# A straight-line schedule for a diffusion block: two heads projected inside the first stage, heads two deep, Fourier products between halves of the output projection

## What is computed

```python
sh1, sc1, gt1, sh2, sc2, gt2 = modulation(c, w_ada[l], b_ada[l])
csh1, csc1, ...              = modulation(c_ctx[None], w_ada[l], b_ada[l])
hc = modulate(rms_norm(ctx, g_mix_pre[l]), csh1, csc1)
uf_c, xc_c, ug_c = mixer_inputs(hc, w_in[l], ...)      # projection 2048 -> 3072, conv of 4 taps
hf_c, hb_c = bi_rglru(xc_c, *lru_p, None, None)        # 8 heads of 128, two directions
hx = modulate(rms_norm(x, g_mix_pre[l]), sh1, sc1)
uf_x, xc_x, ug_x = mixer_inputs(hx, w_in[l], ...)
hf_x, hb_x = bi_rglru(xc_x, *lru_p, hf_c[:, -1], hb_c[:, 0])
y_x = mixer_output(uf_x, hf_x, hb_x, ug_x, w_f, b_f, w_out)   # 4 Fourier groups of 256 + 8 heads, @ w_out
x = x + gt1 * rms_norm(y_x, g_mix_post[l])
hx2 = modulate(rms_norm(x, g_ffn_pre[l]), sh2, sc2)
x = x + gt2 * rms_norm(conv_ffn(hx2, w_up, conv_w, conv_b, w_down), g_ffn_post[l])
```

## Time and profile before

| | |
|---|---|
| median of 3 executions | 2305.04 us (2303.04 to 2308.56) |
| the profiled execution's own time | 2306.21 us |
| its span in the trace | 2304.3 us |
| mean granted TensorE clock | 0.970 |
| PE busy | 2148.7 us (93%) |
| DVE busy | 1316.6 us (57%) |
| ACT busy | 711.2 us (31%) |
| moved by DMA | 301.46 MB, 131 GB/s over the span |

### The profile page before, as it was taken

The page is one execution under the profiler, slowest core; times in us unless marked ns, Lnnn a source line. Parts: engine busy times, 40 slices in busy tenths (PEclk is TensorE's granted clock), DMA queues, the critical chain, the costliest instruction groups (busy, mean ns, idle before and its releaser), DMA issues.

```text
span 2304.3 us, 26994 instructions
## 1 busy us (share of the span) xinstructions
PE 2148.7 (93%) x9608; PEld 1712.4 (74%) x9608; DVE 1316.6 (57%) x1934; ACT 711.2 (31%) x929; POOL 0.2 (0%) x4
## 2 busy tenths in 40 slices
PE   5669999898999789999999999999999999999994
PEld 0058888788877468888888888888888888888883
DVE  4468888987889884434344344434444343434447
ACT  2236656523222333222222223222221222223222
POOL 0000000000000000000000000000000000000000
PEclk8979999999999889999999999999999999999997
DMA  9844334454787432232223222322232223222321
GB/s 378 307 140 149 114 124 146 139 189 146 244 278 271 137 113 97 93 107 92 92 95 103 94 91 93 101 98 91 91 105 95 91 91 102 98 91 91 100 82 73
DMA packets 102137, 301.46 MB, mean 131 GB/s; under 512 B 11344, under 2 KB 11472, under 8 KB 100816
## 3 DMA queue, kind: packets, MB, share of 16 engines
q1 hardware_dynamic: 102096, 300.93, 38.7%
HBM read 296.69 MB, written 4.19 MB: 131 GB/s over the span
## 4 chain that ended last, share of the span: by engine, by line
PE 69%; DVE 19%; DMA 8%; issue 3%; ACT 1%; DVEq 0%; SPq 0%; ACTq 0%
PE bank L648 22%; PE bank L649 22%; PE bank L650 22%; DVE ada_acc L965 5%; DMA ada_raw<-in_adabg 4%; DMA w_raw<-in_ada 4%; DVE w_lo L1047 3%; PE bank L668 1%; DVE xc L1060 1%; DVE lru_i L1070 1%; DVE lru_u L1107 1%; DVE lru_i L1103 1%; DVE x L1269 0%; DVE x L1355 0%; DVE acc L1353 0%
## 5 line engine op out<-in xcount | busy, mean ns | idle before, releaser
L648 PE MATMUL bank<-h_hi,w_hi 128*128 128x512 f32 x2048 | 808.3, 395 | 47.6 <-DVE w_lo L1047 33.0
L649 PE MATMUL bank<-h_lo,w_hi 128*128 128x512 f32 x2048 | 805.1, 393 | 0.0
L650 PE MATMUL bank<-h_hi,w_lo 128*128 128x512 f32 x2048 | 804.5, 393 | 0.0
L1047 DVE TENSOR_TENSOR w_lo<-w_raw,w_hi 128x1024 fp32r<-128x1024 f32 x344 | 405.8, 1221 | 581.8 <-ACT w_hi L388 581.8
L388 ACT ACTIVATE w_hi<-w_raw 128x1024 fp32r<-128x1024 f32 x344 | 347.2, 1052 | 1148.0 <-PE bank L650 1090.2
L648 PEld LDWEIGHTS bank<-h_hi,w_hi 128*128 128x128 f32 x2048 | 389.4, 190 | 126.0 <-DVE w_lo L1047 34.6
L650 PEld LDWEIGHTS bank<-h_hi,w_lo 128*128 128x128 f32 x2048 | 388.6, 190 | 82.3
L649 PEld LDWEIGHTS bank<-h_lo,w_hi 128*128 128x128 f32 x2048 | 389.1, 190 | 75.3
L648 PE MATMUL bank<-act_hi,w_hi 128*128 128x512 f32 x704 | 278.5, 396 | 0.0
L649 PE MATMUL bank<-act_lo,w_hi 128*128 128x512 f32 x704 | 278.4, 396 | 0.0
L650 PE MATMUL bank<-act_hi,w_lo 128*128 128x512 f32 x704 | 278.4, 396 | 0.0
(11 more groups left out here) (183 smaller groups left out, 1412.1 us busy)
## 6 DMA issues: line engine op xcount, KB each, us to landing
w_raw<-in_stream SPq DMA_DIRECT2D x344, 512.0 KB, 4.2
ada_raw<-in_adabg SPq DMA_DIRECT2D x256, 256.0 KB, 4.1
w_raw<-in_ada SPq DMA_DIRECT2D x64, 512.0 KB, 5.7
x<-in_x_t SPq DMA_DIRECT2D x8, 1024.0 KB, 7.8
out_t<-x SPq DMA_DIRECT2D x16, 256.0 KB, 2.0
c<-in_ctx_t SPq DMA_DIRECT2D x2, 1024.0 KB, 9.1
g_raw<-in_gates SPq DMA_DIRECT2D x8, 256.0 KB, 4.2
y_four<-in_tabs SPq DMA_DIRECT2D x4, 258.0 KB, 4.7
```

Source lines behind the costliest of these rows:

```text
L648: nc.tensor.matmul(out, w, v, start=start, stop=False)
L649: nc.tensor.matmul(out, w, v_l, start=False, stop=False)
L650: return nc.tensor.matmul(out, w_l, v, start=False, stop=stop)
L1047: v.tensor_tensor(w_lo[:, s, :], w_raw[:, s, :], w_hi[:, s, :].bitcast(F32), ALU.subtract).then_inc(lo_done, 1)
```

## The change

It rewrites the order of the whole program and the place of its buffers; what is computed stays the same.

- All loops are gone: every engine's program is a straight line. Each unit has a number, and tables say which unit belongs to which job.
- The ring has **five** slots of raw and hi. `w_lo` lies in the same memory as `w_raw` (`twice`): the remainder overwrites the raw weights. So the load of unit n waits until **PE** has used unit n-5.
- Stage one's conditioning matrix has its own ring of 12 slots. The squares are summed by PE (`ones` product into PSUM), no longer by DVE. The `x_t` and `ctx_t` loads come first.
- Heads 0 and 1 are projected inside stage one: `first_heads(k)` uses feature tile k as soon as it is ready, for `u_x` and `u_g` of both heads, after four products of the next chunk of the conditioning matrix. Their eight units are laid out for it.
- Heads 2 to 7: PE projects head h+2 between the gate products of head h. `xc` and the banks of `u_x` are double.
- The first four Fourier tiles are projected between the gate products of heads 6 and 7. The Fourier products of a group are then mixed with the other Fourier tiles and with the first halves of output tiles 0 to 3 (their head part), whose second halves follow group by group (`out_rest`).
- The rest of the conditioning matrix comes in 8 chunks of 1024 columns: 128 loads of 512 KB, 128 accumulations of 128 x 1024. They have three slots (one in the feed-forward) and are issued by **POOL's** queue, with `x1`, `late_par` and the tables of the Fourier stage. Output tiles 3 to 14 carry 5 or 6 of them each (64 in all), the heads and Fourier stages 32, the feed-forward 32.

```diff
-RING = 4
+RING = 5
+SLOT0 = 8
+UX, UG = {0: (1, 7), 1: (1, 7)}, {0: (0, 6), 1: (0, 6)}
...
+ASLOTS = 3
+ACOL = 1024
+NBG = (6 * D - NADA * 1024) // ACOL
+FFN_ADA = NBG - 2
+ADA_SLOT = (4, 3, 3, 3, 3, 0, 3, 3)
...
+        x0, h_lo = twice(ctx, "x0", "h_lo", [P, KT, L])
+        w_raw, w_lo = twice(ctx, "w_raw", "w_lo", [P, RING, UNIT])
...
         @block.sync
-            def load_unit(rnd, s):
-                    sp.wait_ge(lo_done, rnd * RING + s - 3)
-                sp.dma_start(w_raw[:, s, :], stream[rnd * RING + s]).then_inc(raw_in[s], 16)
+            def load_unit(n):
+                if n >= RING:
+                    sp.wait_ge(*used(n - RING))
+                sp.dma_start(w_raw[:, n % RING, :], stream[n]).then_inc(raw_in[n % RING], 16)
...
+        @block.gpsimd
+            def load_ada(first, stop):
+                for q in range(first, stop):
+                    if q < FFN_ADA * KT:
+                        s = q % ASLOTS
+                        if q >= ASLOTS:
+                            pool.wait_ge(ada_eaten, q - ASLOTS + 1)
+                    else:
+                        s = 0
+                        pool.wait_ge(ada_eaten, q)
+                    pool.dma_start(ada_raw(s), adabg[q]).then_inc(ada_in[s], 16)
...
+            for j in range(4):
+                pool.dma_start(x1[:, 4 * j:4 * j + 4, :], x_t[:, 4 * j:4 * j + 4, :]).then_inc(x1_in[j], 16)
+                load_ada(34 + 8 * j, 42 + 8 * j)
...
         @block.tensor
+            for c in range(NADA):
+                for j in range(4):
+                    if c + 1 < NADA:
+                        for u in range(KT * (c + 1) + 4 * j, KT * (c + 1) + 4 * j + 4):
+                            ada_unit(u)
+                    if j == 0:
+                        turn(c)
+                    first_heads(4 * c + j)
...
+            for h in range(1, HEADS - 2):
+                project_x(h + 2)
+                gates(h, 0)
+                project_gate(h + 2)
+                gates(h, 1)
...
+            project_fourier(7)
+            weights_dft(1)
+            out_half(0)
+            token_dft(0)
+            out_half(1)
+            channel_mix(1)
+            weights_dft(2)
...
+            out_rest(8, 9)
+            token_dft(2)
+            out_rest(10)
+            channel_mix(3)
+            out_rest(11)
+            token_dft(3)
+            out_rest(12, 13)
+            out_rest(14, 15)
...
         @block.vector
+            for h in range(HEADS):
+                v.tensor_tensor(xc_lo[:, :], xc[:, h % 2, :], xc_hi[:, :].bitcast(F32), ALU.subtract).then_inc(xc_split, 1)
+                if h > 0:
+                    input_of(h - 1, 1)
+                    gap(h - 1)
+                v.tensor_tensor(g_lo[:, :], g_raw[:, :], g_hi[:, :].bitcast(F32), ALU.subtract).then_inc(gate_lo, 1)
+                lo(n0 + 4)
+                eat_ada(ADA_SLOT[h] // 2)
+                if h > 0:
+                    finish_head(h - 1)
+                if h + 1 < HEADS:
+                    convolve(h + 1)
...
+            for m in range(KT):
+                add_square(ss1[:, :], sq1[:, m % 2, :], m + 2 * KT, first=m == 0)
+                lo(*AFTER_OUT[m])
...
+                if 4 <= m < 12:
+                    place(m - 4)
+                if 3 <= m < 15:
+                    eat_ada(6 if m % 3 == 0 else 5)
```

More of the change, by code:

```diff
@@ new lines, in _, with out_tile @@
+            hi(54)
+            round_wf(3)
+            hi(55)
+            round_yc(10)
+            round_yc(11)
+            round_p(2)
+            round_m(3)
+            round_eo(6)
+            round_eo(7)
+            hi(56)
+            round_yc(12)
+            round_yc(13)
+            round_p(3)
+            round_yc(14)
+            round_yc(15)
+            def out_tile(m):
+                act.wait_ge(*used(OUT_H[m][1]))
+                b = bank[OUT_BANK[m % 4]]
+                a.activation(tile(acc, m), b[:, :], ACT.Copy).then_inc(y_copied, 1)
+                square(sq1[:, m % 2, :], b[:, :], m + 2 * KT)
@@ new lines, in pair @@
+                act.wait_ge(*used(u + 3))
+                hi(u + 6, u + 7)
+                seed(bank[2 * (p % 2) + 1][:, :], cv[:, :], n + FT, seed_v)
+                act.wait_ge(conv_g, n + 1)
+                a.activation(cg[:, p % 2, :], cg[:, p % 2, :], ACT.Gelu_apprx_tanh).then_inc(ffn_gelu, 1)
+            for c in range(NCH):
+                for p in range(CH):
+                    pair(c, p)
+                    if p == 0 and c > 0:
+                        for n in range(DOWN[c - 1], DOWN[c - 1] + KT // 2):
+                            act.wait_ge(*used(n))
+                            hi(n + 4)
@@ new lines, in ada_unit @@
+            def ada_unit(u):
+                k, s = u % KT, u % A0SLOTS
+                pe.wait_ge(a0_in[s], 16 * (u // A0SLOTS) + 16)
+                if k == 0 and u > 0:
+                    pe.wait_ge(rows_copied, u // KT)
+                for part in range(2):
+                    g = 32 * (2 * (k % 2) + part)
+                    mm = t.matmul(bank[5][g:g + 2, :], csil[:, 2 * k:2 * k + 2], ada0_raw[:, s, 512 * part:512 * part + 512],
+                                  start=k < 2, stop=k >= KT - 2, tile_position=(0, g))
+                mm.then_inc(a0_used, 1)
@@ new lines, in project_fourier @@
+            def project_fourier(n):
+                for which in range(2):
+                    half(bank[UF_BANK[n]][:, :], UF[n] + which, which)
+            project_gate(2)
+            pe.wait_ge(mod_made, NADA)
+            gates(0, 0)
+            project_x(2)
+            gates(0, 1)
+            for h in range(1, HEADS - 2):
[3 more added lines that the diff above has]
+                gates(h, 1)
+            pe.wait_ge(xc_done, 7)
@@ new lines, in _ @@
+            out_half(2)
+            token_dft(1)
+            out_half(3)
+            channel_mix(2)
+            weights_dft(3)
+            out_rest(8, 9)
[6 more added lines that the diff above has]
+            out_rest(14, 15)
+            for m in range(4, KT):
+                pe.wait_ge(sq_done, m - 4 + 2 * KT + 1)
+                for which in range(2):
+                    half(bank[OUT_BANK[m % 4]][:, :], OUT_H[m][which], which)
+                if m in SUM_AFTER:
+                    sum_ada(SUM_AFTER[m], bank[2])
@@ L862, in down, with up_pair @@
-            def down(c, rnd, at=0):
-                if at == 0:
+                t.matmul(bank[5][:, :], ones, sq1[:, k % 2, :], start=k == 0,
+                         stop=k == KT - 1).then_inc(x1_summed if k < KT - 1 else totals, 1)
+            def up_pair(c, p):
+                n, u, b = c * CH + p, UP[c, p], 2 * (p % 2)
+                if n > 1:
+                    pe.wait_ge(conv_v, n - 1)
+                for i in range(2):
+                    for which in range(2):
+                        half(bank[b + i][:, :], u + 2 * i + which, which)
@@ L977, in _ @@
             v.memset(eps[:, :], EPS)
+            dve.wait_ge(pos_in, 16)
+            for k in range(0, KT, 4):
+                dve.wait_ge(x_in[k // 4], 16)
+                v.tensor_tensor(*positions(x0, pos0, k, 4), ALU.add).then_inc(x_posed, 1)
             dve.wait_ge(exp_lam, 1)
@@ L1183, in fourier_output @@
[L1183 removed]
+                    v.tensor_tensor(tile(y_four, n, C + 1, L), cosine[:, C - 1:0:-1], b[:, C - 1:0:-1], ALU.add).then_inc(yf_read, 1)
+                dve.wait_ge(yf_read, 2 * g + 2)
                 clear_odd()
[L1186 to L1193 removed]
@@ L1265, in _ @@
             dve.wait_ge(x_posed, 12)
+            chain.wait()
             for k in range(KT):
```

1443 lines of the change are left out of this document (730 added, 713 removed).

## The result

The changed kernel took 2278.41 us (median of four, 2277.27 to 2282.84) beside 2304.04 us for the one before on the same chip (2302.61 to 2308.56): a ratio of 0.9889, 95% interval 0.9870 to 0.9908. It is faster by 26 us, where 78 were forecast; the time lies 18 us above the range.

What follows compares the result with a forecast made beforehand. PE bounds the feed-forward (62% of the span, full clock); other stages are less full. 700 us to the token total + 37 + 24.2 + (1438.8 - 7.5 + 2) + 30.3 = 2225 us span, 2226 us time; range 2200 to 2260.

Steps and rivals of the forecast that it cites:

- 13.0 us a tile: Output tiles 4 to 15: DVE, waiting for three-slot refills, takes 8.9 us for 5.33 blocks plus 4.1 us other work.
- The refill: Output tiles 4 to 15: reloading a conditioning slot by POOL takes 4.2 us to landing plus 0.4.
- PE's 11.7 us: Output tiles 4 to 15: PE needs 10.9 us a tile plus 0.8 for its share of wide sums.
- the hidden refills: Rival, output stage: refills under about 3 us let PE set 11.7 us a tile, total 2207; chance 0.22.
- POOL's loads start late: Rival, output stage: refills wait for one DVE instruction's end, 14.3 us a tile, 2242 (two instructions 2258); chance 0.17.
- 24 us from about 25 us: Stage one, chunk 0: units at 1.5 us with their context squares, starting when x is in and squared; done at 49.5.
- 3 us of stall because a round is now only 26 us: End of the heads, Fourier tiles between gate products: 3 us of stall within the forecast end at 410 us.
- the -7.5: Start of feed-forward: PE's 4.8 us wait behind DVE accumulations and the slow first fourteen products both go, -7.5 us.
- the +2: Feed-forward: two wide sums instead of two narrow ones cost 2 us more.
- the five-slot ring "nothing": Feed-forward: a slot is done within about 9 us and wanted 21.8 us after release, so the ring costs nothing.
- the starved ring: Rival, feed-forward: loads waiting for PE's use starve it, 0.33 us for each of 264 units, about 2313; chance 0.04.
- The order stalls: Rival, 350 to 540 us: about forty hand-overs stall 0.6 us each, 25 us more, total 2250; chance 0.14.

Runs made afterwards that it cites:

- e1: Changed kernel with the sums of chunks 2, 3 and 4 one output tile later on PE and read one tile later by DVE: 2268.69 us.
- e11: Changed kernel with a fourth slot for the output stage's conditioning blocks, sums left where the change put them: 2254.11 us.
- e5: e1 with a fourth slot for the conditioning blocks, from block 36 on: 2244.90 us.
- e6: e1 with the output stage's conditioning loads cut to 8 of 1024 columns, accumulations whole, so the modulation isn't right: 2234.64 us.
- e3: Changed kernel with the residual's four 1 MB loads and the table of positions issued by SP instead of POOL: 2278.97 us.
- e8: e1 with the residual's loads issued by SP: 2264.88 us.
- e12: e10 with the residual's loads issued by SP: 2207.06 us.
- e2: Changed kernel with the output stage's conditioning loads and accumulations cut from 1024 columns to 8 (each chunk's first accumulation stays wide): 2228.63 us.
- e9: Changed kernel with squares added up on DVE, chunk rows turned early, sums one tile later and a fourth slot together: 2215.71 us.
- e10: e9 with ACT taking the gelus of heads 0 and 1 ahead of head 0's seeds and two roundings: 2210.82 us.

## Why the prediction was wrong, step by step

**The step that failed most is "13.0 us a tile" for output tiles 4 to 15.** It set DVE's pace beside PE's and took the slower. Three things were wrong in it.

- *The hand-over at the sum was missing.* I had priced the wide sums as "0.8 us a tile" of PE and not asked what PE waits for before them. The table puts the sum of chunk 2 behind tile 6 and its last block into DVE's step for tile 5. By my own 13.0 and 11.7 us PE would have stood there for about 4 us (an estimate: three steps against three tiles); in the run DVE was only beginning that step when PE had ended tile 6, because its step for tile 3 started late and two steps took 15 us each. Moving the sums gave 9 to 10 us (e1, e11), the low clock behind the idle time with it. That is much less than the 32 us of PE's idle time, since DVE's pace is the next bound.
- *The refill was mis-sized*: 4.6 us, of which 4.2 for landing. In the output stage the blocks landed in 5.0 us in the middle and 9.3 at most, and DVE's step came to 14.2 us (e1) where I had 13.0 (from the accumulation's end to POOL's issue it is 0.3 us, taken as 0.4). With 5.0 + 0.3 in place of 4.2 + 0.4 my own sum gives 13.7 us (an estimate); the last 0.5 us no run places. A fourth slot gave 24 us (e5, e11), and 8-column loads, landing in 2.0 us, another 10 (e6).
- *Loads on the same queue were left out.* The 1 MB loads of the residual stand in POOL's queue among the blocks; I named them in the change and gave them no term. It is 0 to 4 us (e3, e8, e12), so a small slip.

What was right in it: PE's 11.7 us (e2, 11.7 measured), and DVE's work below that (e6). Of my rivals the hidden refills, 2207, is what the stage does when its refills are hidden, but this kernel does not hide them. "POOL's loads start late" gave 14.3 us a tile, the size that e1 shows, from a cause that is not there: that agreement is luck. POOL's issues behind a run of three accumulations on DVE that starts at 631.56 and has one every 1.4 us:

```profile
633.13 0.53 POOL L342 DMA_DIRECT2D ada_raw<-in_adabg  x1 [9.19 <-DVE ada_acc L1053]
633.65 0.53 POOL L368 DMA_DIRECT2D x<-in_x_t  x1
634.52 0.53 POOL L342 DMA_DIRECT2D ada_raw<-in_adabg  x1 [0.34 <-DVE ada_acc L1053]
635.91 0.53 POOL L342 DMA_DIRECT2D ada_raw<-in_adabg  x1 [0.86 <-DVE ada_acc L1053]
```

The first accumulation ends at about 632.8 and POOL issues at 633.13, the second at about 634.2 and POOL at 634.52, while DVE is in the next: 0.3 us each time, no instruction waited out. The Trainium skill's "SBUF — State Buffer", "SBUF: two separate sides", says that DVE in a two-port mode can keep a POOL-issued load from writing its descriptors; I had expected this to bite seldom, and in these rows it does not show. The 3.2 us for such a load, which the prediction estimated by the Trainium skill's "DMA: Bandwidth & Descriptors", "Anatomy of one DMA", are short of the measured 3.7 at least and 5.0 in the middle.

**Stage one: 14.1 us too short.** (The terms of its sum give 161 us, not 162.) "24 us from about 25 us": the squares of x occupied PE to 30.0, since each cost 1.08 us on PE, which I never priced; I had them done as the loads came in. The trace of the kernel before had the price, in its one sum of x's squares over the partitions:

```profile
68.41 1.10 PE L657 MATMUL bank<-ss_x,par 128*128 128x512 f32 x2
```

The units then ran at 1.59 us against my 1.5, and from the last unit to the first feature tile it was 15.0 us (54.8 to 69.8) against 12.5: there PE's first unit of chunk 1 waits 4.9 us for ACT's copy of the rows, behind roots and roundings, and the turn stands behind four such units. That is the 7.8. Behind it the chunk starts were right in size (4.0 us against 4.3) and the four units beside a feature tile too (1.9 us). From one chunk start to the next it was 29.5, 28.5 and 32.7 us (69.8, 99.3, 127.8, 160.5) where I had 28.4 for each; the last one holds a wait of 3.5 us for a remainder that I had not seen. That the loads don't set this stage held, down to e9: both gains of stage one came in full.

**Heads: 7.6 us too short.** The "3 us of stall because a round is now only 26 us" came as forecast: 1.1 us for a late gelu at 390 us and 1.8 at 416 that the profile gives no releaser for. What I had left out is the start: 5.1 us for the first gelu, and behind it some 1.5 us of half clock (products 0.43 us apart from 181.3 to 184.1). e10 gave 5 us back; about 1 us stays unexplained. **Fourier and tiles 0 to 3**: 128 us as forecast. **Norm** 35 us instead of 37, **feed-forward** to the end 1489.4 us against 1487.8: so the -7.5, the +2 and the five-slot ring "nothing" held in their sum, and the starved ring did not come: PE waits for no remainder there. The ring delayed something else: together with the 1 MB load beside it, the unit ahead of tile 3's copy, which landed in time when that load was elsewhere (e3).

**The order stalls** had a chance of 0.14 and 25 us spread over 350 to 540. They came in other places, and larger. As I read it, the range was too narrow because nearly every case priced an engine or a load by itself.

## What to carry to other kernels

When two engines in strict order hand work to each other, compare not only their paces but where each stands: write down, for each wait, how far behind the other engine will be at that moment, since a hand-over placed one step too early can hold an engine for most of a step (8.5 to 13.4 us here), and then costs some clock. How much of that reaches the kernel's time depends on the other engine's pace: here 10 of 32 us. A ring's slots are worth counting against the refill in its *crowded* landing time: with one slot more each load landed later and the stage was still 24 us shorter. And when a sum is moved to another engine "as the data comes", price its instructions there, 32 of them here, before saying that they hide under the loads.
